# Five of 140 weighted additions go to GpSimd, and every eighth tile, taken in plain fp32, starts at tile 0

## What is computed

```python
def block(args):
    xt, it, gt = args
    u = jnp.take(expert_u, it, axis=0)
    act = jax.nn.gelu(jnp.einsum('td,tkd->tk', xt, u)) * gt
    v = jnp.take(expert_v, it, axis=0)
    return jnp.einsum('tk,tkd->td', act, v)
...
h = h + peer(rms_norm(h, ffn_norm_g[l]), ...)
return rms_norm(h, final_norm_g)
```

## Time and profile before

| | us |
|---|---|
| median of 3 runs (3358.7 to 3360.91) | 3360.32 |
| the profiled execution's own time | 3357.68 |
| its span, first to last instruction | 3355.8 |
| stage 1, the dot products, ends | 2932.2 |
| the window: first spike to the first product | 2934.2 to 2959.6 |
| stage 3, the dense product | 2959.6 to 3342.7 |

### The profile page before, as it was taken

One profiled execution on the slowest core, in us unless ns is written; L12 is line 12 of the kernel. 1 busy time (PEld: TensorE's weight loads), 2 busy tenths in 40 slices (PEclk: granted clock), 3 DMA queues, 4 the chain that ended last, 5 costly groups with the idle time before them and its releaser, 6 DMA issues.

```text
span 3355.8 us, 37577 instructions
## 1 busy us (share of the span) xinstructions
PE 2924.4 (87%) x14017; PEld 2381.2 (71%) x14017; DVE 2581.2 (77%) x3901; ACT 1704.3 (51%) x2789; POOL 582.8 (17%) x533
## 2 busy tenths in 40 slices
PE   8999999999999999999999999986654432199998
PEld 7998998888888888888888888852221332177776
DVE  7786767775556787876557685799988899889997
ACT  6554556554445555554445773123443888344444
POOL 0000000000000000000000000555454333335552
PEclk9999999999999999999999999998787555599999
DMA  7554555555555555555556557999999999969997
GB/s 236 163 151 154 161 173 170 172 175 192 189 184 178 189 185 188 188 188 201 188 189 231 168 174 276 336 382 420 417 409 416 422 426 411 390 250 373 382 389 271
DMA packets 424341, 869.08 MB, mean 259 GB/s; under 512 B 18555, under 2 KB 248860, under 8 KB 390624
## 3 DMA queue, kind: packets, MB, share of 16 engines
q1 hardware_dynamic: 347208, 453.16, 40.6%
q0 software_dynamic: 75936, 413.17, 30.7%
q10 hardware_dynamic: 1016, 0.35, 0.0%
HBM read 864.52 MB, written 2.10 MB: 258 GB/s over the span
## 4 chain that ended last, share of the span: by engine, by line
PE 72%; DVE 11%; DMA 9%; issue 3%; ACT 2%; POOL 1%; DVEq 0%; SPq 0%; ACTq 0%; POOLq 0%
PE W L1794 14%; PE W L1802 11%; PE W L1804 11%; PE W L1803 11%; PE W L1792 8%; PE W L1969 7%; DVE Ub L3117 6%; DMA Ub<-in_peer_u,ids 6%; PE T L1965 2%; DMA Vr<-in_peer_v 2%; DMA Vx<-in_peer_v,vid 2%; PE M L1855 1%; DVE X L3177 1%; PE W L1791 1%; PE M L1941 1%
## 5 line engine op out<-in xcount | busy, mean ns | idle before, releaser
L2666 DVE TENSOR_TENSOR wl<-raw,wh 128x1024 fp32r<-128x1024 f32 (+1 forms) x720 | 851.0, 1187 | 563.1 <-ACT wh L2101 561.3
L2101 ACT ACTIVATE wh<-raw 128x1024 fp32r<-128x1024 f32 (+1 forms) x720 | 740.7, 1031 | 893.7 <-PE W L1804 573.7
L1794 PE MATMUL W<-u,wh 128*128 128x512 f32 x2040 | 722.7, 397 | 0.0
L1792 PE MATMUL W<-u,wl 128*128 128x256 f32 x2176 | 603.1, 282 | 0.2 <-DVE u L2628 0.2
L3117 DVE CUSTOM_DVE_ANT_0 Ub<-Ub,W 128x2048 f32<-128x2048 f32 x227 | 514.2, 2284 | 36.6 <-DMA Ub<-in_peer_u,ids 28.1
L1794 PEld LDWEIGHTS W<-u,wh 128*128 128x128 f32 x2040 | 383.3, 188 | 88.4
L1802 PE MATMUL W<-wh,u 128*128 128x512 f32 (+1 forms) x1152 | 436.2, 379 | 1.2 <-DVE u L3026 1.0
L1804 PE MATMUL W<-wh,u 128*128 128x512 f32 (+1 forms) x1152 | 427.9, 371 | 0.0
L1803 PE MATMUL W<-wl,u 128*128 128x512 f32 (+1 forms) x1152 | 427.6, 371 | 0.0
L1792 PEld LDWEIGHTS W<-u,wl 128*128 128x128 f32 x2176 | 410.8, 189 | 6.4 <-issue 0.5
L1941 PE MATMUL M<-Vx,diag 128*128 128x512 f32 x416 | 219.4, 680 | 146.2 <-DMA Vx<-in_peer_v,vid 105.2
(11 more groups left out here) (409 smaller groups left out, 4643.2 us busy)
## 6 DMA issues: line engine op xcount, KB each, us to landing
raw<-in_w_in SPq DMA_DIRECT2D x128, 1024.0 KB, 5.2
raw<-in_w_up SPq DMA_DIRECT2D x88, 1024.0 KB, 4.8
Vr<-in_peer_v SPq DMA_DIRECT2D x128, 512.0 KB
raw<-in_w_down SPq DMA_DIRECT2D x44, 1024.0 KB, 5.0
raw<-in_w_in SPq DMA_DIRECT2D x144, 256.0 KB, 3.4
raw<-in_w_out SPq DMA_DIRECT2D x32, 1024.0 KB, 5.0
raw<-in_w_proj_a SPq DMA_DIRECT2D x16, 1024.0 KB, 5.0
Wb<-in_peer_w_q SPq DMA_DIRECT2D x16, 1024.0 KB, 6.7
```

The lines of the kernel that those rows point to most:

```text
L1792: i = q.matmul(pr[h][:, 0:T], vl, xh, start=False, stop=False)
L1794: i = q.matmul(o, vh, u[:, :, kk, :], start=False, stop=last)
L2101: q.activation(wh[:, s % NS, 0:b.half], r, ACT.Copy).then_inc(s_hi, 1)
L2666: q.tensor_tensor(wl[:, s % NS, 0:b.half], r, wh[:, s % NS, 0:b.half].bitcast(F32), SUB).then_inc(s_lo, 1)
```

## The change

It touches three things. `window_aside` is new: GpSimd itself does the first five additions, each as a TENSOR_SCALAR (side = side * act) and a TENSOR_TENSOR (X = X + side), followed by the gather into the freed buffer. Each of its two instructions counts on the semaphore `s_aside`, which `asides_done` allows for. The other 135 additions start at tile 1 and are spread over 125 tiles. The plain fp32 tiles are 0, 8, 16, ..., 120 (16 of them, as before), and so the two conversions of tile 0 between groups 61 and 62 go.

```diff
-AMID = 0
+WINDOW = 5
...
 def whole_tile(j):
-    return j % RAW == 3
+    return j % RAW == 0
...
+def asides_done(n):
+
+    return n + min(n, WINDOW)
...
         for i in range(ASIDES):
+            if 0 <= i - NA < WINDOW:
+                self.add("window_aside", i - NA)
             self.add("get_aside", i)
         for i in range(48, 64):
             yield lambda: c["DVE"]
             self.add("spike", i)
             self.put("DVE", 1.15, 0.0)
             self.build(i)
-            if i == 61:
-                self.put("ACT", 1.05, 0.0, "high", 0)
-                self.put("DVE", 1.22, 0.0, "low", 0)
...
-        a = self.beside
+        a = WINDOW
         for j in range(128):
             if j:
                 self.add("high", j)
-                self.add("low", j)
+            self.add("low", j)
             self.add("column", j)
-            while a < min(ASIDES, self.beside + (j - 1) * (ASIDES - self.beside) // 120):
+            while a < min(ASIDES, WINDOW + j * (ASIDES - WINDOW) // 125):
                 self.add("aside", a)
                 a += 1
...
                 if i:
-                    e.wait_ge(s_aside, i)
+                    e.wait_ge(s_aside, asides_done(i))
...
                 else:
-                    e.wait_ge(s_aside, i - NA + 1)
+                    e.wait_ge(s_aside, asides_done(i - NA + 1))
...
+            def window_aside(i):
+                t, k = aside_of(i)
+                side = side_b[i % NA]
+                e.wait_ge(*landed("aside", i))
+                e.wait_ge(s_dact, k // GROUP + 1)
+                e.wait_ge(s_rows, 2)
+                q.tensor_scalar(side[:, :], side[:, :], acts[t][:, k:k + 1], None, MUL).then_inc(s_aside, 1)
+                e.wait_ge(s_aside, asides_done(i) + 1)
+                q.tensor_tensor(X[:, t, HALF:D], X[:, t, HALF:D], side[:, :], ADD).then_inc(s_aside, 1)
```

More of the change, by code:

```diff
@@ L1059, in products @@
         self.row_next = 0
-        self.beside = 0
         self.tasks[:] = [task for task in self.tasks if task.rank[1] < 100]
@@ L1979, in mul @@
                         for c in range(2):
-                            m = product(t, c, Ar[a][:, t, :], Vr[j % NT][:, CK[c]], j, 1)
+                            m = product(t, c, Ar[a][:, t, :], Vr[j % NT][:, CK[c]], j, 0)
                     m.then_inc(s_taken, 1)
@@ L2477, in high @@
                 e.wait_ge(s_dot, 256)
-                if j:
+                if v > 1:
                     e.wait_ge(s_built, 64)
@@ L2494, in upper @@
                 if t:
-                    e.wait_ge(s_aside, ASIDES)
+                    e.wait_ge(s_aside, asides_done(ASIDES))
                 else:
@@ L2498, in upper @@
                     e.wait_ge(s_rows, 2)
-                    e.wait_ge(s_aside, 128 - ROWS)
+                    e.wait_ge(s_aside, asides_done(128 - ROWS))
                     e.wait_ge(s_gain, 4)
@@ L3286, in get_aside @@
                 q.indirect_dma_start(side_b[i % NA][:, :], None, ev_half, bass.IndirectOffsetOnAxis(index, 0)).then_inc(s_place[LANDS["aside", i][0]], 16)
-            walk({"setup": setup, "reload": reload, "load_gf": load_gf, "loads": loads,
+            def window_aside(i):
[7 more added lines that the diff above has]
+                q.tensor_tensor(X[:, t, HALF:D], X[:, t, HALF:D], side[:, :], ADD).then_inc(s_aside, 1)
+            walk({"setup": setup, "reload": reload, "load_gf": load_gf, "loads": loads, "window_aside": window_aside,
                   "peer_loads": peer_loads, "get_u": get_u, "get_v": get_v, "get_aside": get_aside})
```

## The result

| | before | after |
|---|---|---|
| median, runs beside each other | 3360.98 (8 runs) | 3372.47 (8 runs, 3368.84 to 3374.11) |
| ratio, 95% interval | | 1.0035 [1.0025, 1.0045] |
| the profiled execution's own time | 3357.68 | 3369.73 |
| its span | 3355.8 | 3367.8 |
| the window, first spike to first product | 25.4 (2934.2 to 2959.6) | 45.5 (2932.1 to 2977.6) |

What follows compares the result with a forecast made beforehand. It took DMA and VectorE, not TensorE, to set the dense stage's pace, with a hole in the window before it. 3357.7 + 3.0 (GpSimd's additions) - 7.0 (stage) = 3353.7, median 2.6 above: 3356.3 us, range 3346 to 3369.

Steps and rivals of the forecast that it cites:

- Step 1: In the window, tile 0's conversions go and spikes run on without the hole: first product at 2953.4, 6.1 us earlier.
- Step 2: Tile 1 waits for GpSimd's five additions, done at 2964.0, and starts at 2966.0; 3.0 us late at tile 3's end.
- my upper bound of 4.5: GpSimd's product and sum of one addition with no streams overlapped: 1.8 and 2.7 us; 3.2 was taken.
- the reload: GpSimd's library reload after its fifth gather, ahead of its first addition: 5.5 us taken.
- The end of GpSimd's work: In the window, GpSimd done with its five additions at 2964.0.
- a sign of being wrong: Prediction wrong if GpSimd's end is off by more than 4 us, or if the stage's idle time stays.
- the forecast's own case: Spikes undisturbed; tile 1 waits for VectorE's sixth addition, TensorE idle 9 us between tiles 0 and 1; chance 0.36.
- the exclusion: Rival, in the window: each GpSimd operation holds the spikes off for its length; + 2.7, or 3363.0; chance 0.22.
- Step 3: In the full stage, five transfers fewer and VectorE's load down to 22.6 us per eight tiles: 7 us less, bounds 2 and 10.
- idle time that stays: TensorE's idle time between 2973 and 3323 was to fall from 11.4 to about 4; staying would show the prediction wrong.
- The sum: Whole kernel: 3357.7 + 3.0 - 7.0 = 3353.7 for the profiled execution; median 2.6 above, 3356.3.

Runs made afterwards that it cites:

- e1: The changed kernel without GpSimd's five additions (WINDOW 0), all 140 on VectorE, spread evenly, plain tiles from 0; 3349.26 us, 0.9965 of the kernel before.
- e9: The same kernel as e1, measured again beside the kernel before; 3349.08 us, ratio 0.9969.
- e7: e1 plus ten GpSimd memsets of 128x1024 into a free buffer in the window; 3356.34 us, 0.9993 of the kernel before.
- e4: The changed kernel with the spikes reading their ramp from PSUM, copied there once by ScalarE; 3364.8 us, 1.0011 of the kernel before.
- e3: The changed kernel with only the even spread: no GpSimd additions, plain tiles and tile 0's conversions as before; 3355.47 us, 0.9982 of the kernel before.
- e2: The changed kernel with only the plain tiles moved: no GpSimd additions, additions spread over 120 tiles as before; 3356.73 us, 0.9988 of the kernel before.
- e6: The changed kernel with GpSimd's five products and sums left out of the computation, early gathers kept; 3347.7 us, 0.9965 of the kernel before.
- e10: The same kernel as e6, measured again beside e9; 3345.75 us, 0.9958 of the kernel before.
- e8: The changed kernel with spikes from PSUM, ScalarE making the five products and GpSimd only the sums; 3350.15 us, 0.9976 of the kernel before.
- e11: Spikes from PSUM and no additions on GpSimd, the base for e8; 3353.26 us, 0.9982 of the kernel before.

## Why the prediction was wrong

- **Step 1 (tile 0's conversions leave the window): right, slightly large.** It gave 6.1 us. e1 and e9 have windows of 20.8 and 20.5 where the kernel before has 25.4, so 4.6 to 4.9 us. The builds took 18.07 and 17.75 us in place of 16.6. Tile 0, plain, lasts 3.7 us to the first product of tile 1 in the change, e1 and e9, in place of 3.0, and the granted clock of the first eight tiles was 1.00.
- **Step 2 (GpSimd's five additions) is the step that failed, twice.** First in its mechanism: it took the spikes to run beside GpSimd undisturbed, and the first product to come at 2953.4 whatever GpSimd did. In fact the spikes were held for 25.2 us, and the place that bound was ahead of tile 0 and not ahead of tile 1. Second in its price: the pair takes 2.87 + 2.35 = 5.2 us, above my upper bound of 4.5 and far above the 3.2 taken. The bound came from a memset, and a memset of the same 1024 elements takes 0.98 (e7), near the 0.95 I worked out; the product of one stream in and one out takes three times that. Against this the reload, taken at 5.5 us between bounds of 1.3 and 10.1, cost at most 0.12. The end of GpSimd's work came out as close to the forecast as it did, 34.3 us after the first spike for 29.8, only by luck: the pairs with their hops were 9.5 us longer in all and the reload 5.4 shorter. Even so, counted from the first spike, it is off by more than the 4 us that the forecast named as a sign of being wrong. e4 shows the forecast's own case, spikes that run free: 1.0011 of before, and still not faster, though there the spikes are 3.8 us slower in all.
- **The rival that held was the exclusion, at a wrong size.** It had 0.22 and gave 3363.0. Its working with the measured pair gives the measured time: 5 x (5.2 - 3.2) = 10 us more make 3373, against 3372.5. That it fits so well is in part luck: tile 0 was put at 5.8 us and lasted 3.7, and the stage behind tile 3 gained 5.0 us and not 7. I had spoken against it with an issue of a gather that runs beside spikes at 0.94 us; but an issue is not one of the operations in question, and the row that bore on it was the one for it, seen from the other side. The Trainium skill (SBUF — State Buffer, the section Who interferes with whom) has this as an exclusive lock between GpSimd and a VectorE instruction in a two-port mode, held for the whole instruction. With operations that read, the runs agree to within a few per cent (9.9 of 10.4, 25.2 of 26.0), with memsets they don't (5.8 of 9.8). In which mode a spike runs no row names.
- **Step 3 (the stage): the size was within its bounds, the reason wrong for the most part.** The stage got 6.1 us shorter. Of that, 1.1 lie in tiles 0 to 3 (12.0 us in place of 13.1), which the forecast counted in its steps 1 and 2, so 5.0 stand against the 7 of step 3, with bounds of 2 and 10. (One transfer comes to 1.37 us by its own figures and not 1.38; nothing hangs on it.) TensorE's idle time did not fall to about 4 us as forecast: it is 9.6, where 11.4 were before, and idle time that stays was named as a sign of being wrong. I put the gain down to five transfers that leave a full DMA. But e1 moves none of them, and its stage is 7.6 us shorter than before (e9: 3.5). By the medians, with the windows taken off, e1 and e9 gain 5.3 and 4.8 us outside the window. What they have is the even spread, which step 3 costed only as a part of VectorE's rate: alone it brings 3.7 us with the window as before (e3), and on top of the plain tile 0 it brings 7.5 (e1 against e2), each with some 3 to 5 us either way. One thing that it changes can be seen at the end, in the 50 us that end some 9 us ahead of the last product. The DMA share was 0.83 there before, where the additions and their gathers had ended by tile 121; in e9 it is 0.92:

```profile
3285.00:3335.00 50.00, 47.62 (x192) 35.57 (x191) 41.23 (x45) 21.79 (x32) 14.82 (x11) 1.00 0.83 315
```

```profile
3276.00:3326.00 50.00, 48.49 (x198) 36.50 (x196) 45.80 (x50) 22.33 (x33) 21.93 (x16) 1.00 0.92 357
```

  The first row is of the kernel before, the second of e9, in the columns of the table by stage. The moved additions themselves bring about 2 us (e6, e10, and e8 against e11), not 7.
- **The sum.** With the window's + 25 for the held spikes, - 5 for tile 0 and - 6 for the stage, the sum is + 14. In the profiled execution the first spike came 2.1 us earlier, which makes the span's + 12.0; the median is + 11.5.

## What to carry to other kernels

An engine that looks idle isn't free to use: before work is moved to GpSimd, look at what VectorE does in that stretch. Where it runs TENSOR_SCALARs on SBUF as here, count GpSimd's busy time in full against them: each moved addition relieved VectorE of 1.28 us and held it for 5.0, on the critical path. Price an operation by a row of the same kind and not by a memset: the product took three times as long as the memset of its size. Of a change in three parts, measure each part: here two parts were worth 0.3% and the third cost 0.7%.

## What was unexpected of the hardware

- A VectorE TENSOR_SCALAR of 128x128 that is held off by GpSimd counts as busy and not as waiting (up to 2.45 us where 0.25 is its pace). It is seen in the mean of its group, 853 ns against 352, and in TensorE's gaps.
- With its one tensor input in PSUM the spike is slower, 0.32 us against 0.26, and it was not held: 20.5 us for 64 with 15.1 us of GpSimd's operations beside them (e4) and 20.5 without (e11).
- GpSimd's product by a per-partition factor, one tensor in, takes 2.87 us for 128x1024, longer than its sum of two tensors, 2.35. ScalarE does the same product in 1.14 us. The Trainium skill (GPSIMD Engine Reference, section 4.1) calls one-input operations there roughly line-rate; by this row, of a product with a per-partition factor, it doesn't hold.
- The reload of the instruction library showed no more than 0.12 us ahead of the first operation. The Trainium skill (GPSIMD Engine Reference, section 2.1) has some 6 us for the first call of a freshly loaded kernel; the trace doesn't agree. Whether anything had to be loaded here, it doesn't show.
- Ten GpSimd memsets of 0.98 us, which only write, held the spikes for 5.8 us in 9.8 (e7).
- GpSimd lost nothing to the spikes: its product and sum took 2.87 and 2.35 us beside spikes from SBUF, and 2.86 and 2.35 beside spikes from PSUM (e4).
